# Unused matrix products in the waits of three stages, and a store issued behind the first input weights, in a two-layer hybrid encoder step

## The chip, the cores and the metric

The kernel runs on one core of one Trainium2 chip. The metric is the device time of one execution in microseconds (us); the median over runs counts. TensorE is called PE here, its weight loads PEld, VectorE DVE, ScalarE ACT, GpSimd POOL and SyncE SP. POOL and SP only issue transfers (DMA) in the stages spoken of.

## The reference

One inference step of a two-layer encoder over 512 prompt tokens and 8 x 16 sample tokens, width 1024, in float32. Cut to what matters:

```python
def _layer(x, c, l, hist, p):
    mod = (jax.nn.silu(c) @ p['w_ada'][l] + p['b_ada'][l]).reshape(B, 6, D_MODEL)
    sh1, sc1, g1, sh2, sc2, g2 = [mod[:, i, None, :] for i in range(6)]
    h = _rmsnorm(x, p['norm_g'][l, 0]) * (1 + sc1) + sh1
    mix, st = _token_mixers(h, l, hist, p)   # mLSTM | indexed sparse attention | pooling
    x = x + g1 * mix
    h = _rmsnorm(x, p['norm_g'][l, 1]) * (1 + sc2) + sh2
    ffn = _swiglu(...) if l % 2 == 0 else _moe(...)   # 8 experts, top 2
    return x + g2 * ffn, st
# in the attention: score = sum_j w_j * relu(q_idx . k_idx); sel = top_k(score, n_sel)
# logits = q . k[sel] / 8 + rel_bias[bucket(distance)]; softmax; @ v[sel]
```

The product of the conditions with `w_ada` (2 x 1024 x 6144) gives the modulation vectors. The relative bias by distance is a table of 8 heads.

## The kernel before

Every engine has its own hand-written stream; semaphores join them, and each engine passes a barrier at the end of each stage. The stages are `ada`, and per layer `z` (input projection), `mlstm`, `index` (scores and top-k selection of the sample tokens), `prompt_att`, `sample_att`, `out` and the feed-forward part.

**Modulation weights.** `w_ada` is read in 48 chunks of 1 MB through the same ring of four slots (`weight_ring`) as all other weights, in the order in which SP issues them. Eight chunks belong to the first stage (`ADA_FIRST`), five and three to the index stages, the rest to the attention stages (`ADA_LATER`). For a chunk PE runs `ada_products` (8 products of 32 output rows and 256 columns, four of them side by side on the array; the trace shows each float32 product as two records, so x16); ACT copies the result to a row buffer, and `ada_turn` turns it with small products (9 columns). The first products of a turn or of the next chunk release the ring slot, and with it the next transfer. In the first stage stand between the chunks `bias_products` (the bias by distance, which ACT writes to `BROW`), after chunk 5 `sums_of_squares` (products with one column, for the norm) and after chunk 6 `spread_roots` (the roots, spread over the partitions).

**The bias rows.** When ACT has written all of `BROW`, POOL stores it to `bias_rows` in DRAM (2.5 MB), waits until it has landed (`bias_out`), and reads the sample tokens' part back (`bias_s`). ACT and DVE wait for `bias_out` in the z stage, after their part of splitting the hidden state and before they evict the first result. From `bias_rows` POOL later loads the heads of the prompt attention.

**First input weights.** The z stage works on weights split into an upper and a lower part: ACT rounds a chunk into `z_weights_upper` and signals `weights_rounded`; DVE subtracts and writes `weights_lower`. The first rounding follows directly on the first stage's barrier.

**Prompt attention.** The loop over `u` runs 16 units (4 head pairs x 4 tiles of 128 queries). At step `u` PE makes the scores of unit `u`, then `ada_turn` of the chunk of step `u - 1`, then claims banks 4 and 5, takes `probs_ready` of unit `v = u - 2` and turns its probabilities, then multiplies those of unit `u - 3` with the values, then runs `ada_products` for the next chunk.

**Fillers.** `fill(bank, n)` runs `n` bfloat16 products of 128x128 by 512 columns whose result nobody reads. The kernel before has them in the mlstm stage (three ahead of two waits per tile) and one at a time in the sample attention. PE runs its stream in order, so a filler stands ahead of the wait that follows it in the code.

Of the kernel before, what the change touches and what calls it, by code (L numbers as in the profile page):

```python
# [199 lines left out]
def build(nc, a, c, o, d):  # L200
# [5 lines left out]
    BF16 = mybir.dt.bfloat16  # L206
# [5 lines left out]
    with ctx:  # L212
        def sb(name, shape):
            return ctx.enter_context(nc.sbuf_tensor(name, shape, F32))

        def sem(name):
            return ctx.enter_context(nc.semaphore(name))
# [12 lines left out]
        ident = sb("ident", [P, P])  # L230
# [31 lines left out]
        FILL_X = ident[:, 0:HD].bitcast(BF16)  # L262
# [40 lines left out]
        _, DENSE_PRODUCT, _, SG = r(NF, HALF), r(NF, HALF), r(2, SLOT), r(2, HALF)  # L303
# [3 lines left out]
        _, _, _, PRODUCT, SGM = r(FE), r(6, FE), r(2 * NF, P), r(FE), r(FE)  # L307
# [5 lines left out]
        _, XR, ACTR, GR_RIDERS, YB_RIDERS = r(2 * KD, P), r(KD, RIDERS), r(3, P), r(D), r(D // 4)  # L313
# [24 lines left out]
        _, DM = g(MH, P, parts=MH), [g(MH, P), tail[3](MH, P)]  # L338
# [9 lines left out]
        QM, _, RL = MQM, g(2 * NB * P + 512), g(2, TP)  # L348
# [27 lines left out]
        NTS, _ = g(P), g(2 * TP)  # L376
# [38 lines left out]
        _, HI_IN_SCRATCH = z(SCRATCH - 3 * FE), z(3, FE)  # L415
# [11 lines left out]
        _, HI_IN_REGION, ACTH, ACTL = r(FE), r(6, FE), r(NF, P), r(NF, P)  # L427
# [21 lines left out]
        PS = ctx.enter_context(nc.psum_tensor("banks", [P, 8, 512], F32))  # L449
# [46 lines left out]
        weights_rounded, weights_split = sem("weights_rounded"), sem("weights_split")  # L496
# [206 lines left out]
        def _(pool):  # L703
            def load(s, *pairs):
                for dst, src in pairs:
                    pool.dma_start(dst, src).then_inc(s, 16)
# [16 lines left out]
            def load_gates(l):  # L723
                load(gates_in, (M0, a["state_m"][l, :, :].rearrange("b h -> h b")),
                     (BGI, a["b_gates"][l, 0:MH].rearrange("(h one) -> h one", one=1)),
                     (BGF, a["b_gates"][l, MH:].rearrange("(h one) -> h one", one=1)))

            load_gates(0)
            pool.wait_ge(bias_row_ready, 1)

            load(bias_out, (bias_rows.rearrange("h p i -> p h i"), BROW[:, :, :]))
            pool.wait_ge(bias_out, 16)
# [190 lines left out]
        def _(pe):  # L923
# [5 lines left out]
            def wait(s, value):  # L929
                pe.wait_ge(s, value)  # L930

            def take(s, inc=1):
                wait(s, n.add(s.name, inc))

            def claim(*banks):
                for b in banks:
                    if holder[b]:
                        wait(*holder[b])
                        holder[b] = None
# [10 lines left out]
            def mm(out, lhsT, rhs, first, last):  # L950
                return nc.tensor.matmul(out, lhsT, rhs, start=first, stop=last)  # L951

            def tr(out, in_):
                k = in_.shape[0]
                return nc.tensor.transpose(out, in_, ident[0:k, 0:k])  # L955
# [7 lines left out]
            def fill(bank, count=1):  # L963

                for _ in range(count):
                    mm(PS[:, bank, :], FILL_X, FILL_Y, True, True)
# [7 lines left out]
            def arrived(q, dmas=1):  # L974
                take(weights_in[q % NSLOT], 16 * dmas)
# [43 lines left out]
            ada_done = 0  # L1019
            rows_out = [None] * 2  # L1020

            def ada_products(bank=None):

                nonlocal q
                bank = ada_done % 2 if bank is None else bank
                arrived(q)
                Wa = WR[:, q % NSLOT, 0:KD * 256].rearrange("p (k n) -> p k n", n=256)
                claim(bank)
                for turn_of in range(2):
                    for g in range(4):  # L1030
                        k = 2 * g + turn_of
                        ins = mm(PS[32 * g:32 * (g + 1), bank, 0:256], CT9[:, k, :], Wa[:, k, :], turn_of == 0, turn_of == 1)
                        if turn_of == 0 and g == 0:
                            free_weights(ins)
                rows_out[ada_done % 2] = hand(ins, "act", bank)
                release[0] = True
                q += 1
# [15 lines left out]
            def ada(rows, count):  # L1053

                nonlocal ada_done
                for c in range(count):
                    ada_done += c > 0
                    ada_products()
                    ada_done -= c > 0
                    if c:  # L1060
                        ada_turn(rows)
                if count:
                    ada_turn(rows)
# [22 lines left out]
            wait(offsets_ready, 1)  # L1086
            for c in range(ADA_FIRST):
                ada_done = c
                ada_products()
                if c:  # L1090
                    ada_done = c - 1
                    ada_turn(ADA_ROWS)
                if c == 1:
                    wait(consts_in, 16 * CONST_LOADS)
                if 1 <= c <= 4:
                    bias_products((c - 1) // 2, c % 2 == 0)
                if c == ADA_FIRST - 3:
                    sums_of_squares("ada", 4)
                if c == ADA_FIRST - 2:
                    spread_roots()  # L1100
            ada_done = ADA_FIRST - 1
# [3 lines left out]
            for l in range(DEPTH):  # L1105
# [71 lines left out]
                for k in range(KD):  # L1177
                    take(z_hidden_split)
                    for name, rows, banks, Wf in lead:
                        if k == 0:  # L1180
# [4 lines left out]
                        _, second = product(PS[0:rows, banks[1], 0:HALF], w, [x[:, k, HALF:] for x in (ZH, ZL)],  # L1185
                                            k == 0, k == KD - 1)
# [5 lines left out]
                for kind, chunk, name, part, banks, who in UNITS[2:]:  # L1192
# [8 lines left out]
                    if kind == "f":  # L1201

                        for k in range(KD):
# [3 lines left out]
                            _, second = product(PS[0:rows, banks[1], 0:HALF], w, [x[:, k, HALF:] for x in (ZH, ZL)],  # L1207
                                                k == 0, k == KD - 1)
# [137 lines left out]
                for u in range(PAIR_UNITS + 3):  # L1346
                    if u < PAIR_UNITS:
                        pair, t = divmod(u, NTP)
                        w = P * (t + 1)
                        b = 2 * (u % 2)  # L1350
                        claim(b, b + 1)
                        for half in range(2):
                            mm(PS[:, b + half, 0:w], ident_masks[:, :], MASK_P[:, sel_at(t):sel_at(t) + w], True, False)
                        for half in range(2):
                            at = slice(half * HD, (half + 1) * HD)
                            ins = mm(PS[:, b + half, 0:w], AQ[at, pair, tiles(t)], AK[at, pair, 0:w], False, True)
                            if turned:
                                ins.then_inc(probs_turned, 1)
                                turned = False
                        hand(ins, "dve", b, b + 1)  # L1360
                    if 1 <= u <= ADA_LATER[l]["prompt_att"]:
                        ada_turn(PROMPT_ROWS, 7)
                    v = u - 2
                    if 0 <= v < PAIR_UNITS:
                        t = v % NTP
                        claim(4, 5)
                        take(probs_ready)
                        for half in range(2):
                            for j in range(t + 1):
                                ins = tr(PS[:, 4 + half, tiles(j)], LG[v % 3][:, half, tiles(j)])  # L1370
                        pts[v] = hand(ins, "act", 4, 5)
                        turned = True
                    v = u - 3
                    if v >= 0:
                        pair, t = divmod(v, NTP)
                        b = 6
                        if t == 0:
                            claim(b)
                        wait(*pts[v])
                        for j in range(t + 1):  # L1380
                            for half in range(2):
                                hd = 2 * pair + half
                                ins = mm(PS[half * HD:(half + 1) * HD, b, tiles(t)], AV[:, j, hd * HD:(hd + 1) * HD],
                                         PT[:, v % 2, half, j, :], j == 0, j == t)
                                if turned:
                                    ins.then_inc(probs_turned, 1)
                                    turned = False
                        ins.then_inc(pv_done, 1)
                        if t == NTP - 1:
                            hand(pe.drain(), "act", b)  # L1390
                    if u < ADA_LATER[l]["prompt_att"]:
                        ada_products(7)
# [14 lines left out]
                for u in range(NB + 2):  # L1407
                    v = u - 2
# [28 lines left out]
                    v = u - 1  # L1437
# [400 lines left out]
                for it in range(4):  # L1838
# [35 lines left out]
                    for j, blocks in enumerate(W2_CHUNKS):  # L1874
                        c = len(UP_CHUNKS) + j
# [1586 lines left out]
```

## Time and profile before

| | |
|---|---|
| median of 3 runs | 2183.32 us (2183.02 to 2191.04) |
| the profiled execution | 2189.17 us |
| its span on the core | 2187.5 us |
| PE busy | 2027.0 us (93% of the span) |
| DVE, ACT busy | 1287.7 us, 1016.2 us |
| granted TensorE clock, mean over the span | 0.953 of full |

Times of rows are microseconds from the span's start. A timeline row gives the start, the length, the engine, the line, the operation, what is written from what, the shape and the number of instructions merged into the row; in brackets stands how long the engine was idle ahead of it and what ended that. The length of a PE row runs to the modelled end of the last product, a little past the start of the next row. The granted clock is 1.00 (2.4 GHz) or 0.50 (1.2 GHz); between them it is a mean over a stretch.

### The profile page before, as it was taken

What the parts mean: (1) busy time and instruction counts of PE and PEld (TensorE: products, weight loads), DVE (VectorE), ACT (ScalarE), POOL (GpSimd) and SP (SyncE); (2) the same over time, 40 slices, a digit from 0 to 9 for tenths busy, and PEclk for the clock granted to TensorE, in tenths of its full rate; (3) what the DMA queues carried; (4) which work ended last, traced back from release to release, by engine and by line L of the source; (5) the groups of instructions that cost most, each with busy time, mean ns of one, the idle gap of its engine ahead of it and who ended that gap; (6) DMA issues with size and microseconds to landing.
All of it is one profiled execution on the core that took longest, in us unless ns stands there. A gap on an engine that the chain in (4) does not pass through costs nothing.

```text
span 2187.5 us, 36988 instructions
## 1 busy us (share of the span) xinstructions
PE 2027.0 (93%) x14437; PEld 1709.7 (78%) x14437; DVE 1287.7 (59%) x2036; ACT 1016.2 (46%) x1528; POOL 180.5 (8%) x271
## 2 busy tenths in 40 slices
PE   6999978898999999998999788988899999999996
PEld 4999845588999999998999545866666667788883
DVE  2657643355544544456666643556565667789885
ACT  5522235543433433335222455435445566677782
POOL 3000120110000000000000021111010010010102
PEclk7999878998999999999999889989999999999998
DMA  9221588532645364552122366217677789899995
GB/s 329 72 78 58 157 227 293 181 130 74 174 127 165 119 173 140 159 152 81 60 77 85 72 234 203 89 52 272 217 267 238 256 281 337 333 370 370 375 384 189
DMA packets 272096, 418.25 MB, mean 191 GB/s; under 512 B 21214, under 2 KB 216312, under 8 KB 271952
## 3 DMA queue, kind: packets, MB, share of 16 engines
q1 hardware_dynamic: 249984, 349.50, 48.5%
q0 software_dynamic: 21968, 66.72, 9.5%
q8 instruction: 103, 1.69, 0.3%
q14 instruction: 41, 0.34, 0.1%
HBM read 385.73 MB, written 29.59 MB: 190 GB/s over the span
## 4 chain that ended last, share of the span: by engine, by line
PE 82%; DMA 5%; DVE 5%; ACT 4%; issue 2%; ACTq 0%; DVEq 0%; POOL 0%; PEldq 0%; SPq 0%; PEld 0%; POOLq 0%
PE banks L951 78%; PE banks L955 4%; DMA expert_ring<-in_we 3%; DMA weight_ring<-in_w_ada 1%; ACT scratch L1911 1%; DVE scratch L2566 1%; DVE region L2566 1%; DVE weights_lower L2566 0%; DMA scratch<-bias_rows 0%; ACT region L1911 0%; ACT region_split L1911 0%; ACTq L1926 0%; ACT hidden_t L1911 0%; ACT mix_t L1911 0%; DVEq L2559 0%
## 5 line engine op out<-in xcount | busy, mean ns | idle before, releaser
L951 PE MATMUL banks<-upper_parts,region_split 128*128 128x320 f32 x1664 | 391.3, 311 | 4.5 <-DVE upper_parts L2566 4.5
L951 PE MATMUL banks<-upper_parts,weights_lower 128*128 128x320 f32 (+1 forms) x1248 | 387.3, 310 | 0.0
L951 PE MATMUL banks<-region_split 128*128 128x320 f32 (+1 forms) x1264 | 339.5, 332 | 3.8 <-DVE upper_parts L2566 3.8
L2566 DVE TENSOR_TENSOR expert_lower<-expert_ring,region_split 128x1408 fp32r<-128x1408 f32 (+1 forms) x198 | 284.2, 1468 | 88.6 <-PE banks L951 64.5
L951 PEld LDWEIGHTS banks<-upper_parts,region_split 128*128 128x128 f32 x1664 | 285.5, 189 | 4.8 <-issue 4.8
L1911 ACT ACTIVATE region_split<-expert_ring 128x1408 fp32r<-128x1408 f32 (+1 forms) x198 | 242.5, 1256 | 59.3 <-DMA expert_ring<-in_we 58.9
L951 PEld LDWEIGHTS banks<-region_split 128*128 128x128 f32 x1264 | 223.4, 188 | 20.1 <-issue 4.3
L951 PEld LDWEIGHTS banks<-upper_parts,weights_lower 128*128 128x128 f32 (+1 forms) x1248 | 235.6, 189 | 0.0
L951 PE MATMUL banks<-region_split,upper_parts 128*128 128x384 f32 x732 | 226.8, 380 | 0.0
L2566 DVE TENSOR_TENSOR weights_lower<-weight_ring,region_split 128x2048 fp32r<-128x2048 f32 (+2 forms) x72 | 168.9, 2350 | 96.6 <-ACT region_split L1911 96.5
L1911 ACT ACTIVATE region_split<-weight_ring 128x2048 fp32r<-128x2048 f32 (+2 forms) x72 | 140.6, 1959 | 164.4 <-PE banks L951 162.8
L1911 ACT ACTIVATE region<-banks 128x320 f32<-128x320 f32 (+4 forms) x178 | 78.4, 460 | 268.8 <-PE banks L951 265.2
L951 PE MATMUL banks<-expert_lower,upper_parts 128*128 128x384 f32 x528 | 197.7, 374 | 0.0
L951 PE MATMUL banks<-z_weights_upper,upper_parts 128*128 128x256 f32 (+2 forms) x644 | 193.1, 334 | 0.1
L951 PE MATMUL banks<-region_split,weights_lower 128*128 128x320 f32 x608 | 188.4, 310 | 0.0
L2566 DVE TENSOR_TENSOR expert_lower<-expert_ring,z_weights_upper 128x1408 fp32r<-128x1408 f32 (+1 forms) x99 | 141.8, 1441 | 71.9 <-PE banks L951 44.2
L951 PE MATMUL banks<-upper_parts,z_weights_upper 128*128 128x320 f32 (+1 forms) x544 | 171.2, 315 | 11.2 <-DVE hidden_lower_parts L2566 10.1
L951 PE MATMUL banks<-hidden_lower_parts,z_weights_upper 128*128 128x320 f32 (+1 forms) x544 | 170.1, 313 | 0.0
L951 PEld LDWEIGHTS banks<-region_split,upper_parts 128*128 128x128 f32 x732 | 135.9, 188 | 32.4 <-issue 10.8
L1911 ACT ACTIVATE z_weights_upper<-expert_ring 128x1408 fp32r<-128x1408 f32 (+1 forms) x99 | 121.8, 1234 | 67.9 <-DMA expert_ring<-in_we 67.7
L951 PEld LDWEIGHTS banks<-z_weights_upper,upper_parts 128*128 128x128 f32 x644 | 120.4, 188 | 16.9 <-issue 7.6
L951 PEld LDWEIGHTS banks<-upper_parts,z_weights_upper 128*128 128x128 f32 (+1 forms) x544 | 103.0, 189 | 17.5 <-issue 15.3
(336 smaller groups left out, 3241.4 us busy)
## 6 DMA issues: line engine op xcount, KB each, us to landing
expert_ring<-in_we SPq DMA_DIRECT2D x176, 704.0 KB, 7.1
expert_ring<-in_we SPq DMA_DIRECT2D x121, 512.0 KB, 4.5
weight_ring<-in_w_ada SPq DMA_DIRECT2D x48, 1024.0 KB, 8.8
weight_ring<-in_w SPq DMA_DIRECT2D x88, 512.0 KB, 4.7
weight_ring<-in_w_in SPq DMA_DIRECT2D x24, 1024.0 KB, 5.2
weight_ring<-in_w SPq DMA_DIRECT2D x16, 1408.0 KB, 6.2
weight_ring<-in_w_out SPq DMA_DIRECT2D x8, 1024.0 KB, 6.2
y_rows<-residual_t POOLq DMA_DIRECT2D x4, 1760.0 KB, 24.8
```

The lines of the kernel that those rows point to most:

```text
L951: return nc.tensor.matmul(out, lhsT, rhs, start=first, stop=last)
L955: return nc.tensor.transpose(out, in_, ident[0:k, 0:k])
L1911: return nc.scalar.activation(out, in_, f, **kw)
L2566: return v.tensor_tensor(out, x, y, op)
```

## The change

Three places get fillers, and one transfer waits for one thing more. In the first stage PE runs four bfloat16 products of 256 columns ahead of each of the eight chunks. In the index stages (`ada`) it runs three of 512 columns ahead of each of the 5 and 3 chunks. In prompt attention it runs, between the claim of banks 4 and 5 and the wait for `probs_ready`, 20 for the first unit and one for each of the other 15, in both layers. POOL issues the store of the bias rows only after ACT's first rounding.

```diff
             load_gates(0)
             pool.wait_ge(bias_row_ready, 1)
+            pool.wait_ge(weights_rounded, 1)
 
             load(bias_out, (bias_rows.rearrange("h p i -> p h i"), BROW[:, :, :]))
             pool.wait_ge(bias_out, 16)
@@ ada, used by the index stages
                 for c in range(count):
                     ada_done += c > 0
+                    claim(ada_done % 2)
+                    fill(ada_done % 2, 3)
                     ada_products()
@@ first stage
             for c in range(ADA_FIRST):
                 ada_done = c
+                claim(c % 2)
+                for _ in range(4):
+                    mm(PS[:, c % 2, 0:256], FILL_X, ident[:, :].bitcast(BF16), True, True)
                 ada_products()
@@ prompt attention
                         t = v % NTP
                         claim(4, 5)
+                        fill(4, 1 if v else 20)
                         take(probs_ready)
```

PE's stream in the second half of the first stage, before (`group_sums` are the turns, `ones,region` 128x1 the sums of squares, `region,ones` the spread roots):

```order
L951 MATMUL banks<-weight_ring,conditions_t 32x256 x8
L951 MATMUL banks<-group_sums,hidden_t 128x9 x2
L951 MATMUL banks<-ones,region 128x1 x10
L951 MATMUL banks<-weight_ring,conditions_t 32x256 x8
L951 MATMUL banks<-group_sums,hidden_t 128x9 x2
```

The same place in the changed kernel:

```order
L952 MATMUL banks<-ident 128x256 x4
L952 MATMUL banks<-weight_ring,conditions_t 32x256 x8
L952 MATMUL banks<-group_sums,hidden_t 128x9 x2
L952 MATMUL banks<-ones,region 128x1 x10
L952 MATMUL banks<-ident 128x256 x4
L952 MATMUL banks<-weight_ring,conditions_t 32x256 x8
```

Four products over the whole array stand ahead of each chunk; between the chunks nothing else moved.

PE's stream at the third and fourth step of the prompt attention of layer 0, before (`selected_p` and `region` are scores, `group_sums,scratch` the turn of a chunk, the L955 rows the turned probabilities):

```order
L951 MATMUL banks<-group_sums,scratch 128x9 x2
L951 MATMUL banks<-weight_ring,conditions_t 32x256 x8
L951 MATMUL banks<-selected_p,ident_masks 128x384 x2
L951 MATMUL banks<-region 128x384 x2
L951 MATMUL banks<-group_sums,scratch 128x9 x2
L955 MATMUL banks<-ident,weight_ring 128x128 x2
L951 MATMUL banks<-weight_ring,conditions_t 32x256 x8
```

And in the changed kernel:

```order
L952 MATMUL banks<-group_sums,scratch 128x9 x2
L952 MATMUL banks<-weight_ring,conditions_t 32x256 x8
L952 MATMUL banks<-selected_p,ident_masks 128x384 x2
L952 MATMUL banks<-region 128x384 x2
L952 MATMUL banks<-group_sums,scratch 128x9 x2
L952 MATMUL banks<-spread,ident 128x512 x20
L956 MATMUL banks<-ident,weight_ring 128x128 x2
```

The 20 fillers stand behind two turns and two chunks, directly ahead of the first turned probabilities.

POOL's stream at the store, in the changed kernel:

```order
L706 DMA vectors_t<-in_state_m 4x8x1
L706 DMA vectors_t<-in_b_gates 4x1 x2
L706 DMA bias_rows<-region 128x8x640 [waits weights_rounded,bias_row_ready]
```

No transfer changed its place in POOL's order; before, the store waited for `bias_row_ready` alone.

## Rows read from the trace of the kernel before

**Rows 1.** The page: granted clock in 40 slices, and the chain that ended last.
```profile
PEclk7999878998999999999999889989999999999998
...
PE 82%; DMA 5%; DVE 5%; ACT 4%; issue 2%; ACTq 0%; DVEq 0%; POOL 0%; PEldq 0%; SPq 0%; PEld 0%; POOLq 0%
```

**Rows 2.** Sums by stretch: busy time per engine, granted clock, DMA share, GB/s.
```profile
28.80:49.30 20.50, 19.63 (x117) 11.60 (x116) 4.71 (x6) 10.58 (x32) 2.37 (x4) 0.50 1.11 348
...
281.50:291.70 10.20, 9.94 (x107) 7.52 (x106) 4.99 (x15) 7.54 (x30) 0.00 (x0) 0.50 0.80 227
308.70:332.70 24.00, 13.95 (x80) 6.84 (x80) 6.56 (x26) 4.17 (x17) 10.01 (x16) 0.50 1.06 355
342.90:353.10 10.20, 8.00 (x50) 5.00 (x54) 3.27 (x12) 3.46 (x11) 0.00 (x0) 0.50 1.04 339
```

**Rows 3.** Timeline of PE, second half of the first stage.
```profile
35.30 1.93 PE L951 MATMUL banks<-weight_ring,conditions_t 128*32 128x256 f32 x16
37.16 1.02 PE L951 MATMUL banks<-group_sums,hidden_t 128*128 128x9 f32 x4
38.04 4.41 PE L951 MATMUL banks<-ones,region 128*128 128x1 f32 x20
...
45.11 2.48 PE L951 MATMUL banks<-region,ones 128*128 128x512 f32 x4
...
49.39 1.19 PE L951 MATMUL banks<-group_sums,hidden_t 128*128 128x9 f32 x8
```

**Rows 4.** Timeline of SP, and its DMA issue: KB, us from issue to landing.
```profile
28.66 2.39 SPq L595 DMA_DIRECT2D weight_ring<-in_w_ada  x1
...
weight_ring<-in_w_ada SPq DMA_DIRECT2D x1, 1024.0 KB, 11.4
```

**Rows 5.** Timeline of POOL at the store, and its DMA issue.
```profile
36.50 0.95 POOL L706 DMA_DIRECT2D bias_rows<-region  x1 [22.40 <-ACTq L1926]
...
bias_rows<-region POOLq DMA_DIRECT2D x1, 2560.0 KB, 11.1
```

**Rows 6.** Timeline of ACT: first rounding, and first eviction of the z stage.
```profile
51.38 0.87 ACT L1911 ACTIVATE z_weights_upper<-weight_ring 128x800 fp32r<-128x800 f32 x1 [0.17 <-ACTq L1929]
...
73.73 0.44 ACT L1911 ACTIVATE region<-banks 100x320 f32<-100x320 f32 x1 [3.98 <-PE banks L951]
```

**Rows 7.** Timeline of PE: fillers that the kernel before has (mlstm).
```profile
289.34 1.46 PE L951 MATMUL banks<-spread,ident 128*128 128x512 bf16 x3
...
293.11 0.82 PE L951 MATMUL banks<-spread,ident 128*128 128x512 bf16 x3
...
1234.72 0.38 PE L951 MATMUL banks<-spread,ident 128*128 128x512 bf16 x1
```

**Rows 8.** Timelines of PE and DVE, end of the index stage, layer 0.
```profile
312.78 1.94 PE L951 MATMUL banks<-weight_ring,conditions_t 128*32 128x256 f32 x16 [5.60 <-DMA weight_ring<-in_w_ada]
...
313.24 0.30 DVE L2728 TENSOR_SCALAR selected_s<-scratch 128x272 bf16<-128x272 f32 x1
```

**Rows 9.** Timeline of PE, prompt attention of layer 0.
```profile
326.56 0.99 PE L951 MATMUL banks<-group_sums,scratch 128*128 128x9 f32 x4 [4.80 <-ACT scratch L1911]
...
332.97 0.42 PE L955 MATMUL banks<-ident,weight_ring 128*128 128x128 f32 x2
...
345.10 1.93 PE L951 MATMUL banks<-weight_ring,conditions_t 128*32 128x256 f32 x16 [3.32 <-DMA weight_ring<-in_w_ada]
...
352.89 1.18 PE L951 MATMUL banks<-weight_ring,conditions_t 128*32 128x256 f32 x16
```

**Rows 10.** Timeline of PE, index end and prompt attention of layer 1.
```profile
1258.53 0.39 PE L951 MATMUL banks<-selected_p,ident_masks 128*128 128x128 bf16 x2 [7.09 <-DVEq L2559]
...
1272.29 0.42 PE L955 MATMUL banks<-ident,weight_ring 128*128 128x128 f32 x2
...
1281.02 1.07 PE L951 MATMUL banks<-weight_ring,conditions_t 128*32 128x256 f32 x16
...
1285.25 0.50 PE L951 MATMUL banks<-selected_p,ident_masks 128*128 128x384 bf16 x2
...
1293.11 0.85 PE L955 MATMUL banks<-ident,weight_ring 128*128 128x128 f32 x6 [1.40 <-DVE weight_ring L2566]
```

## The prediction

> **What bounds the kernel now.** I read the page first. The chain that ended last is 82% PE, and the clock line has dips in its first slices and around slices 5 to 7 and 23 [rows 1]. I then took sums over the stretches in which the clock was at its low level and which the change touches [rows 2]: 28.8 to 49.3 in the first stage, 308.7 to 332.7 across the index stage and the start of prompt attention of layer 0, and 342.9 to 353.1 inside that attention. Together 54.7 us at 1.2 GHz. Last came the timelines of PE, to see which wait ends last in each stretch, since only work that nothing else holds back gets faster with the clock.
>
> In the first stage PE is the bound from 35.30 on: products, turns, the one-column products of 4.41 us and the spread roots follow without idle time until 49.39 + 1.19 = 50.58 [rows 3]. The last chunk's weights were issued at 28.66 and landed 11.4 us later, at 40.1 [rows 4], long before PE came to them. At the end of the index stage of layer 0 the bound is a transfer: PE idles 5.60 us until 312.78; DVE's selection ends at 313.5 [rows 8]. In layer 1 it is DVE: PE idles 7.09 us at the barrier [rows 10]. In prompt attention PE waits 4.80 us at the **second** step, at the turn of a chunk, because ACT stands behind the first softmax. When it reaches the first turned probabilities at 332.97 there is no idle time ahead of them [rows 9], and none in layer 1 at 1272.29 [rows 10].
>
> **Price of a filler.** Three take 0.82 us and one 0.38 us at full clock, so one more costs (0.82 - 0.38) / 2 = 0.22 us; at the low clock three take 1.46, and I take twice 0.22, 0.44 us [rows 7]. One of 256 columns is half of that, so four cost 0.44 or 0.88 us.
>
> **First stage.** Halving the 50.58 - 35.30 = 15.3 us would save 7.6 us; three groups of fillers stand in it (chunks 5, 6, 7), 1.3 us. Best: -6.3 us. If the clock stays low, the groups cost 3 x 0.88: +2.6 us. The five groups before 35.30 lie beside work of ACT and arrivals that pace this part; I cost them at nothing, and at 0.44 us for each one that is exposed. Can fillers hold the clock? The mlstm stage speaks against trusting it: with two groups of three fillers per tile the clock was at 0.50 for all of 281.5 to 291.7 [rows 2, 7]. For it speaks that here the share of fillers is larger. But the change puts none into the 4.41 us of one-column products; I expect the clock to be held until there, to fall behind them, and to come back with the spread roots. Full clock for half of the stretch's work gives -3.8 us; the one-column products, all of them run before the fall, give 1 us more than their half; the three groups of fillers, at mixed prices, cost 1.8 us. -3.8 - 1.0 + 1.8 = **-3 us**, between -6.3 and +2.6.
>
> **The store.** It waits for ACT's rounding, 51.38 + 0.87 = 52.25 now, near 49 then, instead of 36.50 [rows 5, 6]. It takes its 2.5 MB out of the time in which DMA is full (share 1.11 [rows 2]), so the first input weights land sooner; by itself that gains nothing, since PE ends the stage. It lets the z stage start early when PE does. Landing takes 11.1 us at least, so 60 to 61. ACT waits for it ahead of its first eviction, where it now idles 3.98 us from 69.75 [rows 6], 66.8 then: 6 us to spare. Behind it on POOL stand the eight small reads, needed only after the z stage. **0 us**; if the transfer shared with three weight chunks took over 17 us, each further one would count.
>
> **Index stages.** Layer 0: three fillers ahead of each of five chunks. The fifth waits for its weights anyway, 5.60 us, and its 0.66 us of fillers lie in that wait. Those ahead of the first two delay the slot's release by 1.3 us; the transfer then lands up to 1.3 us later, unless it is queued behind others. DMA is full just behind it, so I take 0. If the fillers carry the clock to 312.78, the last product (1.94 us) and its turns run at twice the speed and the stage ends 1.5 us earlier: **-1.5 us**, between -1.7 and +1.3. Layer 1: 9 fillers, 2 us, inside the 7.09 us that DVE holds: **0**; without that cover +2.
>
> **Prompt attention, layer 0.** The 20 fillers come after the wait that they look made for. 20 x 0.22 = 4.4 us on PE, 8.8 at the low clock; the clock rose at 332.7, just there, so I add 0.5: +4.9. What is late next is the rest of PE's stream, until it meets its 3.32 us wait at 345.10 for weights that do not depend on it: -3.3. The idle time was followed by a low clock from 342.9; without idle time I expect it to stay high. One step took 352.89 - 345.10 = 7.8 us at the low clock; the same step in layer 1 at full clock takes 1285.25 - 1281.02 = 4.2 us [rows 9, 10]: -3.6. The 15 single fillers: nine in steps without idle time, 2.0 us; six where PE waits for DVE once in four steps, about half hidden, 0.6 us. Sum **+0.6 us**; between -3 and +11.
>
> **Prompt attention, layer 1.** No low clock inside to win back and no weight wait. 4.4 + 0.3, and the single ones: three exposed (0.66), twelve where PE waits 1.40 us for DVE in one of four steps (1293.11 [rows 10]), half hidden, 1.3: less 0.5 for small waits on ACT in between: **+6 us**, between +4 and +11.
>
> **Sum.** -3 + 0 - 1.5 + 0 + 0.6 + 6 = +2.1 us. Each stage's low stretches also shift with the start of the next, a few us either way: I take +1.5. The sum is made against the profiled execution, 2189.17 us for a span of 2187.5, so 2190.7 there. That execution is 5.9 us above the median, inside the runs shown; on the median's scale 2183.32 + 1.5 = 2184.8 us.
>
> **A rule on the clock.** The trace shows 54.7 us of low clock in the touched stretches, of which by the rows above 6.3 + 1.7 + 3.6 = 11.6 us could return at most, because the rest is idle time or a wait for a transfer. The Trainium skill, "TensorE: Matmul & The Clock Gate", section "Terms", prices throttled time as that time times one minus the ratio, which would be 54.7 / 2 = 27 us. The trace disagrees: in 308.7 to 332.7 PE was busy only 13.95 of 24.00 us [rows 2].
>
> **The rivals.**
> - *All low-clock time returns.* Half of 54.7 us, less the fillers that PE cannot hide (4.4 x 2 + 2.6 + 1.5 = 12.9): -14 us, 2169. For it: PE is 82% of the chain. Against it: the transfers at 312.78 and 345.10. Chance 0.03. The page named above is the one that reads so.
> - *The clock is held throughout the first stage* and across the index stage: -6.3 - 1.7 - 0.5 + 4.5 = -4, with a better start of z up to -8, and with both attentions at their lower bounds -12. 2175 to 2179. Chance 0.17, of it 0.04 beyond 0.5%.
> - *The fillers run slow and win nothing.* One mechanism: at 332.4 and 1272.3 the clock is still low and stays so, 8.8 us each, the first stage pays 2.6 and the step behind keeps its low clock: 2.6 + 8.8 - 3.3 + 2.6 + 8.8 + 1.5 = +21 us, 2204. It decides once the clock stays low for all 20. Against it: in layer 0 it rose at 332.7 with far lighter work. Chance 0.07.
> - *The store becomes the wait.* Landing behind 66.8 instead of 61: +1 to +6 us, 2188. Chance 0.04.
> - *Nothing shows*: fillers hidden, clock unchanged, 2183. Chance 0.09.
> - The forecast, -4 to +8 about the median: 0.60.
>
> 0.5% is 10.9 us, about what a measurement of this kernel can tell from no change. Faster by more: 0.03 + 0.04 = 0.07. Slower by more: 0.07, and 0.02 from the upper ends of the attention terms: 0.09. Within: 0.84. The range 2175 to 2194 leaves out the first rival, half of the second's far part, and the third.
>
> **What would show it.** Right: clock 1.00 at least until 35 in the first stage, PE's last turn near 47 to 48, the store at 49; 20 fillers of 4.4 to 5.5 us ahead of the first turned probabilities with no idle time between; the wait at 345 gone, and 1.00 behind it. Wrong: a first stage that ends at 53 (clock not held) or at 44 (held through); fillers ending inside a wait that remains, which would make them free; a new idle time of ACT ahead of its first eviction in z.

## Result, and the profile after

The changed kernel takes 2195.05 us, the median of 20 executions; the kernel before, run beside it 20 times, takes 2187.2 us. The ratio is 1.0028, with an interval from 1.0015 to 1.0041: 6.1 us longer (3.3 to 9.0). It is estimated from all executions of both kernels and not from the two medians, which would give 1.0036. It lies inside the 0.5% that the prediction named as the bound of a change, but it is not nothing. Twenty executions told more of before than the three at hand for the prediction: they lie between 2180.15 and 2196.47 us. On the scale of those three the ratio gives 2183.32 x 1.0028 = 2189.4 us; 2184.8 was forecast, with -4 to +8 us about the median. So the result lies in the forecast's range and near its upper end.

The profiled execution took 2201.36 us for a span of 2199.7 us, 12.2 us more than that of before (2187.5). Part of that is the difference of two executions: the profiled one is the longest of the 20 of the changed kernel, 6.3 us above their median. So I read it by stage. The page first (its clock line, then the chain that ended last), to be set beside [rows 1]:

```profile
PEclk8999879998999999998999889989999999999998
...
PE 83%; DVE 5%; DMA 4%; ACT 4%; issue 2%; ACTq 0%; DVEq 0%; POOL 0%; PEldq 0%; PEld 0%; SPq 0%; POOLq 0%
```

The first slice and the seventh are better by a tenth, the nineteenth is worse by one, the others are unchanged. The sums by stretch, with the stretches of [rows 2] and the same place in layer 1 (busy time of PE, PEld, DVE, ACT and POOL, clock, DMA share, GB/s):

```profile
28.80:49.30 20.50, 18.86 (x154) 10.66 (x146) 4.76 (x7) 11.19 (x33) 0.00 (x0) 0.75 0.99 282
308.70:332.70 24.00, 15.76 (x93) 8.02 (x90) 6.32 (x26) 4.98 (x20) 10.04 (x16) 0.56 1.06 359
342.90:353.10 10.20, 9.69 (x111) 5.97 (x110) 4.46 (x16) 7.54 (x22) 1.06 (x2) 1.00 0.96 321
1257.30:1281.20 23.90, 15.26 (x69) 6.70 (x71) 7.08 (x28) 3.36 (x14) 10.02 (x16) 0.50 1.05 362
```

The first stage got half of its clock back (0.50 before), the attention of layer 0 all of it behind the 20 fillers (0.50 before), the stretch across the index stage of layer 0 almost nothing. The last stretch had 0.71 before, where the stage began 2.5 us earlier; there the clock is lower now. PE's timeline in the first stage, for [rows 3], with POOL's store and its issue for [rows 5] and ACT's first rounding and first eviction for [rows 6]:

```profile
38.93 2.37 PE L952 MATMUL banks<-ones,region 128*128 128x1 f32 x20
41.16 0.60 PE L952 MATMUL banks<-ident 128*128 128x256 bf16 x4
41.69 1.53 PE L952 MATMUL banks<-weight_ring,conditions_t 128*32 128x256 f32 x16
43.15 1.02 PE L952 MATMUL banks<-group_sums,hidden_t 128*128 128x9 f32 x4
44.02 2.48 PE L952 MATMUL banks<-region,ones 128*128 128x512 f32 x4
46.30 1.06 PE L952 MATMUL banks<-ident 128*128 128x256 bf16 x4
...
49.10 1.20 PE L952 MATMUL banks<-group_sums,hidden_t 128*128 128x9 f32 x8
```

```profile
52.57 0.95 POOL L706 DMA_DIRECT2D bias_rows<-region  x1 [38.46 <-ACT z_weights_upper L1918]
...
bias_rows<-region POOLq DMA_DIRECT2D x1, 2560.0 KB, 8.8
```

```profile
51.11 0.87 ACT L1918 ACTIVATE z_weights_upper<-weight_ring 128x800 fp32r<-128x800 f32 x1 [0.17 <-ACTq L1936]
...
73.45 0.44 ACT L1918 ACTIVATE region<-banks 100x320 f32<-100x320 f32 x1 [3.98 <-PE banks L952]
```

The one-column products ran fast, 2.37 for 4.41 us; four fillers took 0.60 us at full clock and 1.06 us behind the fall. But the clock was not held up to them: it was at full level until 35, at 0.58 and 0.54 over 35 to 37 and 37 to 38.9, and at full level again over 38.9 to 41. The stage ends at 50.30, only 0.28 us earlier. The store is issued 16 us later, lands at 52.57 + 8.8 = 61.4, and ACT idles its 3.98 us ahead of the first eviction for PE, not for the store.

PE's timeline over the end of the index stage and the attention of layer 0, for [rows 8, 9]:

```profile
311.78 1.94 PE L952 MATMUL banks<-weight_ring,conditions_t 128*32 128x256 f32 x16 [1.80 <-DMA weight_ring<-in_w_ada]
...
326.04 0.99 PE L952 MATMUL banks<-group_sums,scratch 128*128 128x9 f32 x4 [5.28 <-ACT scratch L1918]
...
333.10 5.56 PE L952 MATMUL banks<-spread,ident 128*128 128x512 bf16 x19 [0.23 <-issue]
338.50 0.38 PE L956 MATMUL banks<-ident,weight_ring 128*128 128x128 f32 x2
...
347.13 1.07 PE L952 MATMUL banks<-weight_ring,conditions_t 128*32 128x256 f32 x16
...
351.54 1.07 PE L952 MATMUL banks<-weight_ring,conditions_t 128*32 128x256 f32 x16
```

The wait of 5.28 us stands at 326.04, **ahead** of a turn, and the 20 fillers (one record of them is missing) stand seven microseconds behind it, with 0.23 us of idle time ahead of them. Against this profile of before their 5.6 us are given back: the wait for weights at 345.10 is gone and the step behind takes 351.54 - 347.13 = 4.4 us. From the turn to that step it is 25.5 us, against 352.89 - 326.56 = 26.3 before.

The same place in layer 1, for [rows 10], and the piece of the chain of waits that runs through it (start, us, what):

```profile
1261.02 0.39 PE L952 MATMUL banks<-selected_p,ident_masks 128*128 128x128 bf16 x2 [4.81 <-DVEq L2566]
...
1269.78 0.99 PE L952 MATMUL banks<-group_sums,scratch 128*128 128x9 f32 x4 [4.07 <-ACT scratch L1918]
...
1276.84 6.42 PE L952 MATMUL banks<-spread,ident 128*128 128x512 bf16 x19 [0.23 <-issue]
1283.10 0.38 PE L956 MATMUL banks<-ident,weight_ring 128*128 128x128 f32 x2
```

```profile
1271.38 5.22 PE banks L952 x26
...
1276.84 6.42 PE banks L952 x19
```

The index fillers shorten the wait for DVE from 7.09 to 4.81 us and cost nothing. The 20 lie on the chain itself. The first turned probabilities come 10.8 us later than in the profile of before (1283.10 for 1272.29), of which 2.5 us were there when the stage began and 3.4 us at the turn (1269.78 for 1266.42); the 7.4 us from the turn on are the fillers and the low clock that they met. Nothing behind gives them back. Part of this is not the fillers' doing: the clock stays low here in e4 and g1 too, which have no fillers in this attention. From this turn to the fourth chunk behind it they take 1286.42 - 1269.21 = 17.2 and 1276.62 - 1259.54 = 17.1 us, where before takes 1281.02 - 1266.42 = 14.6. So about 2.5 of the 7.4 us come in some executions without any filler.

### The profile page after: what moved, and what is told of

Same layout as the page of the kernel before. It is cut to its first block, busy times and chain, and to the rows that moved or that the text cites. A ratio compares the mean times of both kernels' runs of the same rounds, so it can differ in the third digit from the quotient of the medians.

```text
span 2199.7 us, 37181 instructions
## 1 busy us (share of the span) xinstructions
PE 2046.8 (93%) x14519; PEld 1721.1 (78%) x14563; DVE 1287.5 (59%) x2036; ACT 1017.2 (46%) x1528; POOL 175.5 (8%) x271
## 4 chain that ended last, share of the span: by engine, by line
PE 83%; DVE 5%; DMA 4%; ACT 4%; issue 2%; ACTq 0%; DVEq 0%; POOL 0%; PEldq 0%; PEld 0%; SPq 0%; POOLq 0%
PE banks L952 79%; PE banks L956 4%; DMA expert_ring<-in_we 2%; ACT scratch L1918 1%; DVE region L2573 1%; DVE scratch L2573 1%; ACT region L1918 1%; DMA scratch<-bias_rows 1%; ACT region_split L1918 1%; ACT hidden_t L1918 0%; ACTq L1933 0%; DVE weights_lower L2573 0%; DMA hidden_t<-h_rows,pass_tokens 0%; DMA weight_ring<-in_w_ada 0%; ACT mix_t L1918 0%
## 5 line engine op out<-in xcount | busy, mean ns | idle before, releaser
L1918 ACT ACTIVATE region_split<-expert_ring 128x1408 fp32r<-128x1408 f32 (+1 forms) x198 | 242.9, 1256 | 62.2 <-DMA expert_ring<-in_we 61.4
```

What stands on the lines that cost most here:

```text
L1918: return nc.scalar.activation(out, in_, f, **kw)
```

## The experiments

Each kernel was timed in five rounds beside the kernel before. That has a median of 2189.53 us (35 executions) beside the e runs, 2189.34 (29) beside the f runs and 2187.52 (35) beside the g runs. All edits are to the kernel before unless said otherwise.

**e1, fillers and store of the first stage alone.**

```diff
             pool.wait_ge(bias_row_ready, 1)
+            pool.wait_ge(weights_rounded, 1)
...
                 ada_done = c
+                claim(c % 2)
+                for _ in range(4):
+                    mm(PS[:, c % 2, 0:256], FILL_X, ident[:, :].bitcast(BF16), True, True)
                 ada_products()
```

> Only the fillers of the first stage and the later store. Theory A (the loss sits in the two prompt attentions): no loss here, -4 to +1 us against the kernel before, ratio 0.998 to 1.0005; the clock is at 1.00 until about 35, low somewhere behind the one-column products, PE's last turn of the first stage between 46 and 51 (50.6 before, 50.3 in the changed kernel). Rival B (the store now collides with the z stage, or the fillers of the first stage cost more than they return): +4 to +7 us here, ratio 1.002 to 1.003, and ACT's first eviction of the z stage later relative to the stage's start.

Measured: 2185.56 us, ratio 0.9981 (0.9961 to 1.0001), -4.2 us: what a stage ended 3 to 4 us earlier would give, though the interval touches 1. In its profile PE's last turn starts at 46.68, and ACT rounds without a wait for weights:

```profile
46.68 1.19 PE L952 MATMUL banks<-group_sums,hidden_t 128*128 128x9 f32 x8
```

```profile
48.73 0.87 ACT L1915 ACTIVATE z_weights_upper<-weight_ring 128x800 fp32r<-128x800 f32 x1 [0.17 <-ACTq L1933]
```

**e2, the 20 fillers alone, in both layers.**

```diff
                         claim(4, 5)
+                        if v == 0:
+                            fill(4, 20)
                         take(probs_ready)
```

> Only the 20 fillers ahead of the first turned probabilities, both layers. Theory A: they stand behind the wait, 4.4 us each at full clock and up to 7 where the clock is low. Layer 0 gives it back (the weight wait at 345 vanishes, the clock stays at 1.00 behind it), 0 us; layer 1 keeps +4.5 to +7. In all +4 to +7, ratio 1.002 to 1.003. Rival B (PE has time to spare there, the fillers are free): 0, ratio 1.000, with idle time of PE left between the fillers and the turned probabilities.

Measured: 2194.87 us, ratio 1.0025 (1.0009 to 1.0042), +5.5 us. This alone is nearly the whole loss. PE's timeline in layer 1, where the clock was at its full level this time, gives the price: 4.48 / 20 = 0.22 us each, with no idle time ahead.

```profile
1268.61 0.61 PE L951 MATMUL banks<-group_sums,scratch 128*128 128x9 f32 x4
1269.08 4.48 PE L951 MATMUL banks<-spread,ident 128*128 128x512 bf16 x20
1273.39 0.38 PE L955 MATMUL banks<-ident,weight_ring 128*128 128x128 f32 x2
```

Its first stage is that of before, and yet PE's last turn starts there at 43.59, not 49.39. ACT then does not profit, because it waits for the first input weights, whose transfer here overlaps that of the early store (a timeline of PE, then of ACT):

```profile
43.59 1.20 PE L951 MATMUL banks<-group_sums,hidden_t 128*128 128x9 f32 x8
```

```profile
48.68 0.87 ACT L1913 ACTIVATE z_weights_upper<-weight_ring 128x800 fp32r<-128x800 f32 x1 [3.25 <-DMA weight_ring<-in_w_in]
```

**e3, the 15 single fillers per layer alone.**

```diff
                         claim(4, 5)
+                        if v:
+                            fill(4)
                         take(probs_ready)
```

> Only the single fillers ahead of the other 15 units, both layers. Theory A: 0.22 us each where PE does not wait; 2.6 us in layer 0, partly lost in the weight wait at 345, 2.0 in layer 1: +2 to +4, ratio 1.001 to 1.002. Rival B (hidden in the drain of the products ahead, or in the waits on DVE): under +1, ratio 1.000. The trace tells it by the length of one step at full clock: 4.2 us before, 4.4 if exposed.

Measured: 2186.42 us, ratio 0.9988 (0.9969 to 1.0007), -2.6 us: the +2 to +4 us of theory A are outside the interval. But the sign named ahead says the opposite: the step below takes 345.45 - 341.04 = 4.41 us, and the same step 346.99 - 342.75 = 4.24 us in e2 and 4.23 us in g1 and g2, which have no single fillers. In such a step a single filler is exposed, by 0.17 us; in the time of the whole kernel this does not show, and the two are not reconciled. Its profile has the wait for the first input weights too, 1.75 us behind a last turn at 45.02. Its attention of layer 0 ran at full clock from 335 us on, with no wait for weights, although the 20 are not there:

```profile
341.04 1.07 PE L951 MATMUL banks<-weight_ring,conditions_t 128*32 128x256 f32 x16
...
345.45 1.07 PE L951 MATMUL banks<-weight_ring,conditions_t 128*32 128x256 f32 x16
```

**e4, the index fillers alone.**

```diff
                     ada_done += c > 0
+                    claim(ada_done % 2)
+                    fill(ada_done % 2, 3)
                     ada_products()
```

> Only the three fillers ahead of each chunk in the index stages. Theory A: hidden in both layers (under 5.60 us of waiting for weights, under 7.09 of waiting for DVE): -1.5 to +0.5, ratio 0.999 to 1.000; the prompt attention of layer 0 starts up to 1.5 us earlier if the clock stays up until the last chunk. Rival B (the later release of the ring slots delays the transfers): its start 1 to 3 us later.

Measured: 2191.02 us, ratio 1.0008 (0.9990 to 1.0026): nothing that can be told from zero. In its profile the clock did stay up until the last chunk of the index stage of layer 0, and PE then waited longer for ACT in the attention:

```profile
310.73 1.07 PE L951 MATMUL banks<-weight_ring,conditions_t 128*32 128x256 f32 x16 [1.40 <-DMA weight_ring<-in_w_ada]
...
323.42 0.99 PE L951 MATMUL banks<-group_sums,scratch 128*128 128x9 f32 x4 [7.29 <-ACT scratch L1913]
```

The next chunk begins 3.4 us behind this one (314.11), where before it is 5.35 (318.13 - 312.78). Of these 2.0 us the turn is left with 1.1: 323.42 - 310.73 = 12.7 us for 13.8.

**f1, forty in place of twenty (e2 with `fill(4, 40)`).** It asks whether their price is linear and exposed.

> 40 fillers in place of 20 ahead of the first turned probabilities, nothing else changed. Theory A (they lie on PE's path in layer 1, and in layer 0 only as far as the wait for weights absorbs them): 20 more cost 4.4 us in each layer at full clock, and nothing is left to absorb them: +8 to +9 us beyond the kernel with 20 alone (+5.5 measured), so +13 to +16 against the kernel before, ratio 1.006 to 1.0075. Rival B (the 5.5 us come from the clock's drift between runs and the fillers are hidden): unchanged at 0 to +5, ratio under 1.0025.

Measured: 2206.25 us (6 executions), ratio 1.0072 (1.0048 to 1.0097), +15.8 us. The 40 further products (20 in each layer) cost 0.0047 x 2189 = 10.3 us over e2, 0.26 us each, with an interval of some 6 us about the 10.3. So they are exposed, and rival B is out; the price of 0.22 us lies inside. One of the two places, from PE's timeline:

```profile
333.62 8.58 PE L951 MATMUL banks<-spread,ident 128*128 128x512 bf16 x39
342.03 0.38 PE L955 MATMUL banks<-ident,weight_ring 128*128 128x128 f32 x2
```

**g1 and g2, the 20 in one layer only** (e2 with `if v == 0 and l == 0`, and with `l == 1`).

> The 20 fillers in layer 0 alone. Theory A (4.4 us on PE's path, given back by the wait for weights that follows some steps later): +4 us at the first turned probabilities, 0 to +1 at the end of that attention, -1 to +2 in the total, ratio 0.9995 to 1.001. Rival B (the 5.5 us of both layers are shared evenly): +2 to +4, ratio 1.001 to 1.002.

> The 20 fillers in layer 1 alone. Theory A (no wait for weights in layer 1, nothing absorbs them): +4.4 to +7, ratio 1.002 to 1.003, and the shift at the first turned probabilities is still there at the end of the attention. Rival B: +2 to +4, ratio 1.001 to 1.002.

Measured: g1 2187.44 us, ratio 1.0003 (0.9986 to 1.0021); g2 2193.27 us, ratio 1.0024 (1.0007 to 1.0040), +5.2 us. The two together, +5.9, repeat e2. By these times layer 0 shows no cost and layer 1 does, but the two intervals overlap, and an even share, rival B, is in both. In the profiles layer 1 keeps its fillers: from the turn to the fourth chunk behind it g2 takes 1279.73 - 1261.37 = 18.4 us and e2 18.6, for the 14.6 of before. In layer 0 the 20 of g1 took 6.1 us, and the steps behind ran at 4.2 us without a wait:

```profile
321.13 1.00 PE L951 MATMUL banks<-group_sums,scratch 128*128 128x9 f32 x4 [4.71 <-ACT scratch L1913]
...
328.19 6.11 PE L951 MATMUL banks<-spread,ident 128*128 128x512 bf16 x19 [0.23 <-issue]
...
342.44 1.07 PE L951 MATMUL banks<-weight_ring,conditions_t 128*32 128x256 f32 x16
...
346.67 1.07 PE L951 MATMUL banks<-weight_ring,conditions_t 128*32 128x256 f32 x16
```

The same turn and the same chunk in g2, whose attention of layer 0 is that of before:

```profile
323.84 0.99 PE L951 MATMUL banks<-group_sums,scratch 128*128 128x9 f32 x4 [4.87 <-ACT scratch L1913]
...
344.83 1.07 PE L951 MATMUL banks<-weight_ring,conditions_t 128*32 128x256 f32 x16
```

That is 21.0 us, without the wait for weights and without the low clock behind it. The unchanged attention of e1 takes 20.3 us, also without them. With them, before takes 352.89 - 326.56 = 26.3 us and e4 27.1 (350.55 - 323.42, behind a wait of 4.40 us). The 20 fillers stand between: 23.1 us in e2, 25.5 in g1 and in the changed kernel. So layer 0 gives its fillers back only against an execution that has the wait; against one without it they cost 2 to 5 us. What decides whether the wait comes is open.

**f2, eight fillers inside the real wait**, ahead of the turn at which PE waits for ACT.

```diff
+                    if u == 1:
+                        claim(4, 5)
+                        fill(4, 8)
                     if 1 <= u <= ADA_LATER[l]["prompt_att"]:
                         ada_turn(PROMPT_ROWS, 7)
```

> 8 fillers, moved to where PE does wait for the first softmax: at the second step, ahead of the turn of the chunk (4.80 us of idle time in layer 0, 3.22 in layer 1). Theory A: they are hidden (1.8 us at full, 3.5 at the low clock) and cost nothing; whether they raise the clock for the 6 us behind the wait decides the gain: 0 to -6 us, ratio 0.997 to 1.000. Rival B (PE's place in the stream does not matter, 8 fillers cost 8/20 of 20): +2, ratio 1.001.

Measured: 2186.82 us, ratio 0.9988 (0.9971 to 1.0006). The seven recorded lie inside the wait and carry the turn to full clock, 0.58 us instead of 0.99. The next product is at 1.94 us all the same, and the wait for weights stands where it stood:

```profile
320.67 1.67 PE L951 MATMUL banks<-spread,ident 128*128 128x512 bf16 x7 [0.16 <-issue]
325.75 0.58 PE L951 MATMUL banks<-group_sums,scratch 128*128 128x9 f32 x4 [3.41 <-ACT scratch L1914]
326.94 1.94 PE L951 MATMUL banks<-weight_ring,conditions_t 128*32 128x256 f32 x16 [0.61 <-ACT modulation_t L1914]
...
344.21 1.94 PE L951 MATMUL banks<-weight_ring,conditions_t 128*32 128x256 f32 x16 [4.04 <-DMA weight_ring<-in_w_ada]
```

By the time (-2.6 us, -6.3 to +1.3) the 8/20 of the price of the 20 that rival B names is just outside the interval. Placed there the fillers cost nothing that shows; a gain is not shown either, and the low clock behind the turn stayed.

**f3, e1 and ten more fillers between the one-column products**, where the clock fell in e1 and in the changed kernel.

```diff
                 claim(bank)
+                if of == "ada":
+                    claim(5)
...
+                    if of == "ada":
+                        mm(PS[:, 5, 0:256], FILL_X, ident[:, :].bitcast(BF16), True, True)
                     mm(PS[:, bank, t:t + 1], SS[:, tiles(t)], ones[:, 0:1], t == 0, False)
...
+                    if of == "ada":
+                        mm(PS[:, 5, 0:256], FILL_X, ident[:, :].bitcast(BF16), True, True)
                     ins = mm(PS[:, bank, t:t + 1], SQ[:, tiles(t)], ones[:, 0:1], False, t == NT - 1)
```

> First stage and store as in the changed kernel, and ten more fillers of 256 columns between the one-column products of the norm, into bank 5. Theory A (in the changed kernel the clock falls because nothing loads the array in the one-column products): the clock stays at 1.00 to the end of the stage, PE's last turn at 45 to 47, and the whole is 1 to 4 us faster than with the first stage's fillers alone: -3 to -8 against the kernel before, ratio 0.9965 to 0.9985. Rival B (the fall has nothing to do with these products): the clock falls all the same, 1.1 to 2.2 us slower than with the first stage's fillers alone.

Measured: 2185.07 us, ratio 0.9985 (0.9965 to 1.0005). The clock stayed at full level and the last turn started at 43.05. But f4 did the same without the ten.

**f4, the changed kernel without the 20** (`if v: fill(4)` in place of `fill(4, 1 if v else 20)`).

> The changed kernel with the 20 fillers of the first unit taken out again, the single ones and everything else kept. Theory A: loses its loss: +6 of the changed kernel less 4 to 7, so -3 to +2 against the kernel before, ratio 0.9985 to 1.001. Rival B (the loss sits in the index stages or in the parts together): still +4 to +7, ratio 1.002 to 1.003.

Measured: 2194.16 us, ratio 1.0012 (0.9994 to 1.0030). By the ratio 3.5 us are gone of the 6.1; with these intervals that agrees with e2, and with a smaller share too. The +2.6 us lie between the two forecasts, and the interval (-1.3 to +6.6) excludes neither. Its profile, at a span of 2177.9 us, shows the first stage at its best (two rows of PE and one of ACT; then the sums of 35 to 45):

```profile
38.20 0.60 PE L952 MATMUL banks<-ident 128*128 128x256 bf16 x4
...
42.89 1.19 PE L952 MATMUL banks<-group_sums,hidden_t 128*128 128x9 f32 x8
```

```profile
44.89 0.87 ACT L1919 ACTIVATE z_weights_upper<-weight_ring 128x800 fp32r<-128x800 f32 x1 [0.17 <-ACTq L1937]
```

```profile
35.00:45.00 10.00, 9.08 (x92) 6.40 (x84) 2.44 (x4) 5.76 (x18) 0.00 (x0) 1.00 0.92 221
```

**g3, f3 without the later store** (all its fillers, the store issued where it was).

> The first stage's fillers with the ten more between the one-column products, and the store where it was (issued when its rows are written). Theory A (the store's 2.5 MB stand ahead of the first input weights, and they become the bound once PE is fast): PE's last turn at 44 to 45 as with the later store, but ACT's first rounding waits 3 to 6 us for the weights and the z stage starts 2 to 5 us later; ratio 0.999 to 1.001. Rival B (the place of the store does not matter): as with the later store, ratio 0.9985, no wait of ACT for a transfer ahead of its first rounding.

Measured: 2188.96 us, ratio 1.0001 (0.9986 to 1.0016). In this profile the clock was low in spite of the ten; sums of 35 to 45, and PE's last turn:

```profile
35.00:45.00 10.00, 10.00 (x74) 7.32 (x74) 1.02 (x2) 4.16 (x14) 0.95 (x1) 0.52 1.10 365
```

```profile
48.86 1.19 PE L951 MATMUL banks<-group_sums,hidden_t 128*128 128x9 f32 x8
```

So neither that the ten hold the clock is shown, nor what the later store is worth by time: f3 and g3 differ by 0.0016 with intervals of that size. The case that g3 was built for, PE early with the store early, did not come in its profile. What it does show is the landing of a small piece of the first input weights, here for g3 and then for f3 (DMA issues: KB, us from issue to landing):

```profile
weight_ring<-in_w_in SPq DMA_DIRECT2D x1, 112.0 KB, 10.1
```

```profile
weight_ring<-in_w_in SPq DMA_DIRECT2D x1, 112.0 KB, 5.0
```

**g4, f3 and f2 together**, the version that the experiments pointed to.

> The two parts that gave the lowest ratios together: the first stage with ten more fillers and the later store, and 8 fillers ahead of the first turn of the prompt attention. Theory A (they are in different stages and add up): 0.9985 and 0.9988 give 0.9973, -6 us, 0.9955 to 0.999. Rival B (the 8 fillers do nothing, their ratio was the clock's drift): 0.9985, as with the first stage alone.

Measured: 2188.81 us, ratio 1.0003 (0.9986 to 1.0020). The 0.9973 of theory A is outside the interval: the two do not add up, or one of the two low ratios was chance. No version tried is surely faster than before; the best single ones are e1 and f3, both with 1 just inside their intervals.

## Why the prediction came out as it did

- **Price and place of the 20: right.** 4.48 us for 20 was forecast at 4.4. That they stand behind the wait and not in it is shown by e2 and f1, where the time rises with each of them.
- **Layer 0, +0.6: right in size** (-0.8 from the turn to the step behind in the profile, g1 +0.7 us with an interval from -3 to +5), **in part by luck.** With the fillers in, the wait at 345.10 and the low clock behind it go, as forecast. But the two terms that pay for the fillers, -3.3 and -3.6, were read from one execution. In e1, e3 and g2, where no 20 stood in this attention, the wait and the low clock are gone too (20.3 to 21.9 us from the turn to the step behind, for 26.3). There is then nothing to win back, and the 20 cost 2 to 5 us.
- **Layer 1, +6: right.** Of it 4.7 us are the 20; g2, which has only them, shows +5.2 (1.5 to 8.7). In the profiled execution it was +7.5 (1283.10 - 1269.78 = 13.3 us, 1272.29 - 1266.42 = 5.9 us before, by the start of the same turn), since the clock was low when the fillers began: about 7 us for the 20 in place of 4.7. About 2.5 us of the +7.5 come with the low clock alone, as e4 and g1 show.
- **First stage, -3: mis-sized in the profiled execution, -0.3, and about right over several.** The mechanism came in part: full clock through the one-column products and the fall behind them, but the clock was already low over 35 to 38.9, ahead of them. It is not shown to be the fillers' work either, since the unchanged first stages of e2 and e3 have the same 2.37 us of one-column products and a fall behind them. The clock came back only with the last turn, not with the spread roots: these took 2.48 us, as in [rows 3], where f4 had them in 1.33, and the fillers and products behind them ran slow as well. ACT's first rounding starts at 47.0 us on average in the five profiles with fillers and the later store (51.11, 48.73, 44.89, 45.05 and 45.21) and at 50.2 in the eight without both; e1 gives -4.2 us. A difference of 3 us between sets that each spread over 4 to 6 us supports the size and does not fix it. It belongs to fillers and store together: the later store takes away a wait that the first input weights put there.
- **The store, 0: right as far as it goes.** It never became a wait. In the changed kernel it landed in 8.8 us, where the forecast had "11.1 us at least". It is also not idle: where PE ends early, the early store costs ACT 3.25 (e2) and 1.75 us (e3) of waiting for weights, and in none of the five profiles with the later store is there such a wait. A piece of 112 KB of the first input weights shows the cause: it lands in 9.9 to 10.2 us in all nine kernels with the early store and in 4.8 to 5.2 us in all five with the later one, g3 and f3 among them, which differ in the store alone. Its gain is only had where PE ends early; by time it was not measured alone.
- **Index stages, -1.5 and 0: near in size, not by the mechanism.** The term for layer 0 wanted the fillers to carry the clock through the wait to the last chunk. In the profiled execution it fell in the wait of 1.80 us, and the last chunk took 1.94 us as before. PE's step after the selection began 1.0 us earlier (316.08 for 317.08) because the chunk's weights landed 1.0 us earlier. In e4's profile the clock was carried, and 1.1 of 2.0 us were left at the turn that waits for ACT. By time e4 shows nothing.
- **The sum.** Forecast +2.1, taken as +1.5; measured +6.1 (3.3 to 9.0), four times the forecast though inside its range. The part of the loss that experiments pin down, the 20 in layer 1, stands where the working put it. In the profiled execution two terms were mis-sized, the first stage by 2.7 and layer 1 by 1.5 us. Over many executions both come out near their forecast when done alone, and the whole is still dearer than its parts: -4.2 (e1) + 5.5 (e2) - 2.6 (e3) + 1.8 (e4) = +0.5 us, 5.6 us less than measured. Each part has an interval of 3 to 4 us either way. If they are independent, the five intervals together allow 8 to 9 us, so the 5.6 may be nothing. If it is real, it does not sit with the 20: f4, which lacks them, is at +2.6, and its parts (e1, e3, e4) add up to -5.0. The cause, if there is one, is open.
- **"All low-clock time returns": wrong, as forecast.** The mean granted clock of an execution of the changed kernel is 0.9572. The clocks of the executions of before beside it were not recorded; beside the e, f and g runs before has 0.9506, 0.9512 and 0.9522. So the changed kernel has 0.0050 to 0.0066 more, which is 0.0050 x 2190 / 0.5 = 22 to 29 us less time at 1.2 GHz, and it is 6 us longer. Where the regained clock stands was not counted out; the fillers and the waits are the places that the profiles offer. (The Trainium skill, "TensorE: Matmul & The Clock Gate", section "Terms", would count half of those 22 to 29 us as won; the times here do not agree.)
- **The other rivals.** A first stage at full clock throughout came in the profiles of f3, f4 and g4, so it happens, but it did not carry the time of f4 below that of before. The slow fillers came in half: in layer 1 they met the low clock, in layer 0 the wait of the profile of before was gone.

## What to carry to other kernels

A filler is free only inside the wait that it is meant for: find in the engine's timeline the instruction that carries the idle time, put the filler ahead of that one, and where it stands behind, price it as work. A wait that is to give its price back must be there in more than one execution. A higher mean clock is no gain by itself; ask which of the regained stretches the next engine was waiting for. Where executions of one program differ by 0.9%, a term of 3 us is judged by several profiles and a few dozen executions, never by one trace beside one trace.

## What the runs showed of the hardware

The granted clock differs from execution to execution in code that is the same. The first stage of before, run unchanged in before, e2 and e3, had its last turn at 49.39, 43.59 and 45.02 us, with clocks of 0.50, 0.76 and 0.75 over 28.8 to 49.3. Over the 35 executions of before beside the e runs the mean clock lay between 0.947 and 0.956 and the time between 2179.90 and 2198.93 us; a line through them gives -1.6 us per 0.001, with a correlation of -0.8, about two thirds of the variance. If every low stretch lay in PE's bound work, 0.001 would be 0.001 x 2187 / 0.5 = 4.4 us at half speed, so 2.2 us; the fitted 1.6 is somewhat below that.

The ten fillers between the one-column products cost little at full clock: from the start of the first to the start of what follows, the 20 products with ten fillers took 38.36 - 35.88 = 2.5 us in f3, against 38.20 - 35.97 = 2.2 us for the 20 alone in f4. By the price of 0.11 us for one filler of 256 columns the ten would be 1.1 us.
